# The modulation of a diffusion layer joins the first FFN: two sections ahead of x, six made beside the products

## The reference

```python
mod = (silu(c) @ ada_w + ada_b).reshape(1, 9, 1024)        # once with c_ctx, once with c; ada_w is 1024 x 9216
h = rmsnorm(x, norm_w[0]) * (1.0 + m[1]) + m[0]
x = x + 0.5 * m[2] * swiglu(h, ffn1_w13, ffn1_w2)          # (silu(h @ a) * (h @ b)) @ d, hidden width 2816
h = rmsnorm(x, norm_w[1]) * (1.0 + m[4]) + m[3]
x = x + m[5] * token_mixer(h)                              # projection, RWKV-7 scans, Fourier mixing, merge
h = rmsnorm(x, norm_w[2]) * (1.0 + m[7]) + m[6]
x = x + 0.5 * m[8] * swiglu(h, ffn2_w13, ffn2_w2)
```

## Time and profile before

| | us |
|---|---|
| median of the runs shown | 3244.37 (3243.7 to 3245.0) |
| profiled execution, its own time | 3243.18 |
| span of its profile | 3241.4 |
| PE busy | 2975.2 (92%) |
| DVE busy | 1456.3 (45%) |
| ACT busy | 776.3 (24%) |
| POOL busy | 332.4 (10%) |

### The profile page before, as it was taken

One profiled execution on the slowest core, in us unless ns is written; L12 is line 12 of the kernel. 1 busy time (PEld: TensorE's weight loads), 2 busy tenths in 40 slices (PEclk: granted clock), 3 DMA queues, 4 the chain that ended last, 5 costly groups with the idle time before them and its releaser, 6 DMA issues. The chain is left out here.

```text
span 3241.4 us, 56108 instructions
## 1 busy us (share of the span) xinstructions
PE 2975.2 (92%) x23416; PEld 2787.4 (86%) x23416; DVE 1456.3 (45%) x2475; ACT 776.3 (24%) x1296; POOL 332.4 (10%) x318
## 2 busy tenths in 40 slices
PE   4799999999996999998699976989979999999997
PEld 1399999999995988998588954779879999999996
DVE  0344333334436345432688855335553343443335
ACT  0321111111113233443133334212141111111112
POOL 0310000000004001122121212012240000000000
PEclk7899999999998999999799998989999999999999
DMA  9411111111102334443444321242111111111111
GB/s 399 159 40 39 39 39 39 57 50 42 39 13 90 129 107 149 164 156 138 116 109 96 68 107 33 71 172 93 44 36 46 39 39 39 39 39 39 39 40 64
DMA packets 182217, 263.72 MB, mean 81 GB/s; under 512 B 78128, under 2 KB 133424, under 8 KB 177456
## 3 DMA queue, kind: packets, MB, share of 16 engines
q1 hardware_dynamic: 182064, 261.52, 24.5%
HBM read 206.35 MB, written 55.12 MB: 81 GB/s over the span
## 5 line engine op out<-in xcount | busy, mean ns | idle before, releaser
L474 DVE SCALAR_TENSOR_TENSOR x<-bank,gate,x 128x128 f32<-128x128 f32 (+1 forms) x832 | 411.6, 516 | 209.6 <-PE bank L573 209.1
L609 DVE TENSOR_TENSOR g_ffn<-act_out_ffn,bank 128x384 f32<-128x384 f32 x132 | 73.2, 554 | 742.7 <-ACT act_out_ffn L606 742.7
L558 PE MATMUL bank<-h_hi_ffn,wlo_a_ffn 128*128 128x384 f32 x1056 | 356.9, 338 | 21.2 <-DVE h_lo_ffn L325 11.3
L606 ACT ACTIVATE act_out_ffn<-bank 128x384 f32<-128x384 f32 x132 | 65.0, 492 | 1246.1 <-PE bank L558 1246.0
L558 PE MATMUL bank<-h_lo_ffn,whi_a_ffn 128*128 128x384 f32 x1056 | 355.8, 337 | 0.0
L558 PE MATMUL bank<-h_hi_ffn,whi_a_ffn 128*128 128x384 f32 x1056 | 355.5, 337 | 0.0
L573 PE MATMUL bank<-g_hi_ffn,wlo_d_ffn 128*128 128x384 f32 x1056 | 352.9, 334 | 2.4 <-DVE g_lo_ffn L494 2.4
L573 PE MATMUL bank<-g_hi_ffn,whi_d_ffn 128*128 128x384 f32 x1056 | 352.7, 334 | 0.0
L558 PE MATMUL bank<-h_hi_ffn,whi_b_ffn 128*128 128x384 f32 x1056 | 352.7, 334 | 0.0
L573 PE MATMUL bank<-g_lo_ffn,whi_d_ffn 128*128 128x384 f32 x1056 | 352.7, 334 | 0.0
L558 PE MATMUL bank<-h_hi_ffn,wlo_b_ffn 128*128 128x384 f32 x1056 | 352.7, 334 | 0.0
(11 more groups left out here) (236 smaller groups left out, 4915.9 us busy)
## 6 DMA issues: line engine op xcount, KB each, us to landing
ada_raw<-in_ada_w SPq DMA_DIRECT2D x36, 1024.0 KB, 11.6
raw_a_ffn<-in_ffn_w SPq DMA_DIRECT2D x44, 512.0 KB, 4.6
raw_b_ffn<-in_ffn_w SPq DMA_DIRECT2D x44, 512.0 KB, 4.5
raw_d_ffn<-in_ffn_w SPq DMA_DIRECT2D x44, 512.0 KB, 3.6
raw_in<-in_w_in SPq DMA_DIRECT2D x35, 512.0 KB, 5.1
mix<-row_out SPq DMA_DIRECT2D x23, 576.0 KB, 3.1
sc_ar<-streams SPq DMA_DIRECT2D x36, 256.0 KB, 3.5
sc_bkv<-streams SPq DMA_DIRECT2D x36, 256.0 KB, 4.2
```

Source lines behind the costliest of these rows:

```text
L474: ins = nc.vector.scalar_tensor_tensor(xs, kit.banks[4 + d % 4][:, a:b], kit.gate[:, gate, d, cond:cond + 1], xs, ALU.mult, ALU.add)
L558: mm = nc.tensor.matmul(kit.banks[2 * slot + j][:, 0:CH], w[q][:, par, cols], v[:, k, toks], start=(k == 0 and m == 0), stop=(k == ku - 1 ...
L606: return self.nc.scalar.activation(out, a, ACT.Silu)
L609: self.nc.vector.tensor_tensor(g32, act_out, b, ALU.mult).then_inc(g32_ready, 1)
```

## The change

The stage `modulation` goes. A class `Opening`, a `Norm` with the modulation in it, takes its place in the first FFN alone; other stages are built as before.

- SP: vectors, select, section 0, section 1, x, a and b of the first tile, section 2, and (behind a wait for section 2's row products) d of the first tile.
- Sections 0 to 2 are made as before, by row products, copies and turns. Squares start when both first sections are turned (the rows lie in the squares' buffer), each waiting for its pair of x blocks. ACT's order is: squares of chunk 0, root 0, the first weights, squares of chunk 2, roots 1 and 2, then h for all chunks. The row products of section 2 stand behind the column sums, its turn behind the first up step.
- Sections 3 to 8 don't use the row products. POOL makes them in 24 units, one for each section and quarter of 256 columns: `acc[p, cond, col]` is the sum over k of `raw[p, col] * silu[p, k, cond]`, 8 multiplications and 7 additions of 128x512. POOL issues its own loads, 128 KB each (192 in all, two buffers, two ahead). There are four sum buffers. In pairs 3 to 8, behind up (0, 2) and up (1, 0), PE sums two quarters each over the partitions, with one-column matmuls against ones into free columns of bank 7, and DVE adds the bias for the pair's section behind up (1, 0). Behind pair 8 DVE forms the remaining scales and gates.

The core of the diff; buffers and semaphores are left out:

```diff
-def modulation(kit):
...
+class Opening(Norm):
+    QW = D // 4
+    SUMS = {(0, 2): (0, 1), (1, 0): (2, 3)}
+    AT = 384
+    TURN_BANK = (7, 4, 7)
...
+    def load_first(self, sp):
+        kit = self.kit
+        sp.dma_start(kit.vec[:], kit.dram["vec"]).then_inc(self.S["vec_loaded"], 16)
+        sp.dma_start(self.select[:], kit.dram["select"]).then_inc(self.S["select_loaded"], 16)
+        for i in range(2):
+            self.load_section(sp, i)
+        for k in range(KT):
+            sp.dma_start(kit.x[:, k, :], kit.dram["xT"][k]).then_inc(self.x_loaded[k // 2], 16)
+
+    def load_third(self, sp):
+        self.load_section(sp, 2)
+        sp.wait_ge(self.S["mod_rows_done"], 6)
...
+    def tensor(self, pe):
+        pe.wait_ge(self.S["silu_ready"], 4)
+        self.rows_of(pe, 0, (0, 1))
+        self.rows_of(pe, 1, (2, 3))
+        pe.wait_ge(self.S["select_loaded"], 16)
+        self.turn(pe, 0)
+        self.turn(pe, 1)
+        pe.wait_ge(self.S["ones_ready"], 3)
+        pe.wait_ge(self.S["section_added"], 2)
+        super().tensor(pe)
+        pe.wait_ge(self.rms_ready, 3)
+        self.rows_of(pe, 2, (5, 6))
...
+    def sum_up(self, pe, i, quarters, x_added):
+
+        pe.wait_ge(x_added, i * 24)
+        for q in quarters:
+            pe.wait_ge(self.S["unit_ready"], i * 4 + (q - 11))
+            for mt in range(2):
+                for cond in range(2):
+                    at = self.AT + 2 * (2 * q + mt) + cond
+                    mm = self.nc.tensor.matmul(self.kit.banks[7][:, at:at + 1], self.acc[:, q, cond, mt * P:(mt + 1) * P],
+                                               self.kit.ones[:, 0:1], start=True, stop=True)
+            mm.then_inc(self.S["unit_turned"], 1)
...
+    def scalar(self, act, split_weights):
...
+        self.copy_rows(act, 0, (0, 1))
+        self.copy_rows(act, 1, (2, 3))
+        act.wait_ge(S["mod_turned"], 2)
+        self.squares(0, act, 0)
+        act.wait_ge(S["ones_ready"], 3)
+        root(0)
+        split_weights()
+        self.squares(0, act, 2)
+        for c in (1, 2):
+            root(c)
+        act.wait_ge(S["scale_ready"], 1)
+        for m in range(NC * KT):
...
+    def sections(self, pool):
+
+        nc, S, QW = self.nc, self.S, self.QW
+        pool.wait_ge(self.h_ready, NC * KT)
+        pool.wait_ge(S["mod_turned"], 3)
+        pool.wait_ge(S["silu_ready"], 4)
+        units = [(i, q) for i in range(3, 9) for q in range(4)]
+
+        def load(n):
+            u, k = divmod(n, KT)
+            i, q = units[u]
+            pool.dma_start(self.raw[:, n % 2], self.kit.dram["ada_w"][i, k // 2, :, k % 2, q * QW:(q + 1) * QW])\
+                .then_inc(self.unit_loaded[n % 2], 16)
+        load(0)
+        load(1)
+        step = 0
+        for u in range(len(units)):
+            if u >= 4:
+                pool.wait_ge(S["unit_turned"], u - 3)
+            acc = self.acc[:, u % 4]
+            for k in range(KT):
+                n = KT * u + k
+                pool.wait_ge(self.unit_loaded[n % 2], 16 * (n // 2 + 1))
+                if step:
+                    pool.wait_ge(S["unit_step"], step)
+                nc.gpsimd.tensor_tensor(self.product[:] if k else acc,
+                                        self.raw[:, n % 2:n % 2 + 1].broadcast_to([P, 2, QW]),
+                                        self.silu[:, k].rearrange("p (c t) -> p c t", t=1).broadcast_to([P, 2, QW]),
+                                        ALU.mult).then_inc(S["unit_step"], 1)
+                step += 1
+                pool.wait_ge(S["unit_step"], step)
+                if n + 2 < KT * len(units):
+                    load(n + 2)
+                if k:
+                    ins = nc.gpsimd.tensor_tensor(acc, acc, self.product[:], ALU.add).then_inc(S["unit_step"], 1)
+                    step += 1
+            pool.wait_ge(S["unit_step"], step)
+            pool.sem_inc(S["unit_ready"], 1)
...
@@ def hidden_stage
+            if opening:
+                opening.load_first(sp)
+            for q in "ab":
                 load(q, 0, True)
+            if opening:
+                opening.load_third(sp)
+            load("d", 0, True)
...
                         up(i, par, c, early)
+                        if opening and early and (par, c) == (0, 0):
+                            opening.third_turn(pe)
+                        if beside and (par, c) in opening.SUMS:
+                            opening.sum_up(pe, i, opening.SUMS[par, c], x_added)
+                        if opening and (early or beside) and (par, c) == (1, 1):
+                            pe.wait_ge(opening.S["section_added"], 3 if early else i + 1)
                         if (par, c) in DOWN:
...
         with kit.stage():
-            modulation(kit)
-        with kit.stage():
-            ffn(kit, "ffn1", 0, "ffn1_w13", "ffn1_w2")
+            ffn(kit, "ffn1", 0, "ffn1_w13", "ffn1_w2", first=True)
```

More of the change, by code:

```diff
@@ L379, in hidden_stage @@
             moving = [(norm_part.h_hi, norm_part.h_lo)] * 2
+            opening = norm_part if norm_part.opens else None
         else:
             norm_part = None
[L382 to L384 removed]
+        g_hi1, g_lo1 = buf("g_hi1", [P, NC, CH], F32R), buf("g_lo1", [P, NC, CH], F32R)
+        if opening:
+            opening.beside(buf)
+        elif norm_part:
             buf("past_scratch", [P, norm_part.scratch_width - 2 * NC * CH])
@@ L387, in hidden_stage @@
         raw = {q: buf(f"raw_{q}", [P, width[q]]) for q in "ab"}
+        whi, wlo = ({q: buf(f"{n}_{q}", [P, 2, width[q]], F32R) for q in "ab"} for n in ("whi", "wlo"))
+        if opening:
+            with ExitStack() as scratch:
+                opening.third(scratch)
+        g_hi, g_lo = [buf("g_hi0", [P, NC, CH], F32R), g_hi1], [buf("g_lo0", [P, NC, CH], F32R), g_lo1]
         raw_d = buf("raw_d", [P, ahead, D])
         raw_of = lambda q, slot: raw_d[:, slot % ahead] if q == "d" else raw[q][:]
-        whi = {q: buf(f"whi_{q}", [P, 2, width[q]], F32R) for q in kinds}
-        wlo = {q: buf(f"wlo_{q}", [P, 2, width[q]], F32R) for q in kinds}
+        whi["d"], wlo["d"] = buf("whi_d", [P, 2, D], F32R), buf("wlo_d", [P, 2, D], F32R)
         act_out, g32 = buf("act_out", [P, 2, CH]), buf("g32", [P, 2, CH])
@@ L405, in load @@
                     combine.load(sp, f, slot, first, g32_ready)
-            for q in kinds:
+            if opening:
+                opening.load_first(sp)
+            for q in "ab":
                 load(q, 0, True)
+            if opening:
+                opening.load_third(sp)
+            load("d", 0, True)
             if load_x:
@@ L486, in step @@
                                g32[:, slot], g32_ready)
+                if opening and early and (par, c) == (0, 2):
+                    opening.third_gate(dve)
                 if (par, c) in DOWN:
@@ L506, in _, with pair @@
                 first_weights()
-            def pair(i, early=False, last=False):
+            def pair(i, early=False, last=False, beside=False):
                 for par in range(2):
@@ L511, in pair @@
                         step(i, par, c, early, last)
+                        if beside and (par, c) == (1, 0):
+                            opening.add_section(dve, i)
             pair(0, early=True)
-            with dve.Fori(1, pairs - 1) as i:
-                pair(i)
+            if opening:
+                with dve.Fori(1, 3) as i:
+                    pair(i)
+                with dve.Fori(3, 9) as i:
+                    pair(i, beside=True)
+                opening.finish(dve)
+                with dve.Fori(9, pairs - 1) as i:
+                    pair(i)
+            else:
+                with dve.Fori(1, pairs - 1) as i:
+                    pair(i)
             pair(pairs - 1, last=True)
@@ L522, in _ @@
                 norm_part.pool(pool)
+            if opening:
+                opening.sections(pool)
             if not combine.on_pool:
@@ L575, in down, with pair @@
                     mm.then_inc(down_done, 1)
-            def pair(i, early=False):
+            def pair(i, early=False, beside=False):
                 for par in range(2):
@@ L585, in _ @@
             pair(0, early=True)
-            with pe.Fori(1, pairs) as i:
-                pair(i)
+            if opening:
+                with pe.Fori(1, 3) as i:
+                    pair(i)
+                with pe.Fori(3, 9) as i:
+                    pair(i, beside=True)
+                with pe.Fori(9, pairs) as i:
+                    pair(i)
+            else:
+                with pe.Fori(1, pairs) as i:
+                    pair(i)
             down(pairs - 1, NC - 1)
```

190 lines of the change are left out of this document (188 added, 2 removed).

## The result

| | median of the runs | profiled execution | span |
|---|---|---|---|
| before | 3244.68 us (3243.7 to 3245.76, 4 runs) | 3243.2 us | 3241.4 us |
| after | 3334.66 us (3331.56 to 3335.94, 4 runs) | 3335.9 us | 3334.1 us |

The changed kernel takes 1.0276 times as long (95% interval 1.0258 to 1.0294), 90 us more. The forecast was 3326 us, 82 us more.

A forecast was written before the change was run, and what follows sets the result against it. TensorE, 92% busy, was taken to bound the kernel, with loading limiting its opening. Opening -83.3, GpSimd-paced pairs +163, clock +2 gave +82 on 3243.2: 3325 us, 3326 as median; range 3195 to 3405 for 8 in 10.

The forecast's parts named there:

- The mechanism: Pairs 4 to 8: TensorE stops once per pair, about 30 us, awaiting GpSimd's units; lower clock behind it.
- The opening: Everything before the first product, reordered: first product at 66.0 instead of 149.28 us, saving 83.3 us, 8 us either way.
- t: GpSimd's time for one unit of sections 3 to 8: 27.2 us, from 18.9 to 36.6; break-even 23.1.
- The issue: GpSimd's own DMA issue, eight per unit: 0.85 us each, ends 0 and 1.85.
- the sum: First t's terms, 27.2 us; later the whole forecast: -83.3 + 163 + 2 = +82, 3325 us, median 3326.
- VectorE's disturbance: VectorE's two-input SBUF subtractions slowing GpSimd's units: 1 us on a unit, 0 to 1.5.
- Landings: GpSimd's loads in the units: issued 4.8 us ahead of use, 128 KB landing in 2.4 us, so not late.
- the stretch of the units: Pairs 3 to 8: 20 units take 545.5 us against 382.7 before, 163 more, plus 2 for the clock.
- Keeping up: Rival, pairs 3 to 8: t 18.9 to 20.2, TensorE never stopped, 3183 to 3190 us; keeping up or nearly, 0.25.
- The hold-up of issues: Rival, GpSimd's units: VectorE delays issues to 1.85 us, t 35.2, 3486 us; 0.13 together with slow landing.
- the slow landing: Rival, GpSimd's loads: landing sets the pace; at 6 us, t 32, 3422 us; 0.13 together with held-up issues.
- The late first product: Rival, opening: chunk 0 waits for the last root, first product near 74, 3334 us; no chance of its own.

The follow-up runs named there:

- one_k: The changed kernel with only the first of eight multiplications per GpSimd unit, one load, no additions; sums and waits kept: 3200.74 us, ratio 0.9859 to the kernel before.
- double_issue: The changed kernel with each of GpSimd's 192 loads issued as two halves, same bytes in 384 issues: 3413.79 us, ratio 1.0518 to the kernel before.
- spread_two_k: The changed kernel with three units a pair in pairs 1 to 8, three sum buffers, and 96 loads of 256 KB: 3201.34 us, ratio 0.9864 to before.
- before_split: The kernel before with TensorE's loop over the first FFN's pairs cut into the changed kernel's three loops, nothing added: 3248.19 us, ratio 1.0009.
- before_order: The kernel before with its weight halves laid out in the changed kernel's order: 3246.81 us, ratio 0.9996.

## Why the prediction was right, point by point

**The mechanism was the predicted one.** A stop once a pair in pairs 4 to 8, ahead of the one-column matmuls, none in pair 3 because four units lie ready, the lower clock behind each, and GpSimd without a gap but for its waits. one_k shows that it is GpSimd's work, double_issue that each microsecond of it counts 20 times. The stops themselves are 17 to 25 us and not the 30 forecast, since a pair's excess also holds the sums, the lower clock and the slower up products.

**The opening, -83.3 forecast, -78.6 measured.** The first product stands at 70.57, not 66.0. The timeline of the kernel after shows where:

```profile
29.50 4.73 PE L300 MATMUL bank<-select,square_n 128*128 128x2 f32 x32
34.27 0.94 ACT L128 ACTIVATE square_n<-x 128x384 f32<-128x384 f32 x2 [4.03 <-PE bank L300]
34.93 8.73 PE L140 MATMUL bank<-square_n,ones 128*128 128x384 f32 x20 [0.71 <-ACT square_n L128]
42.46 1.28 ACT L366 ACT_TABLE_LOAD   x1 [2.69 <-PE bank L140]
43.75 0.58 ACT L366 ACTIVATE inv_rms_n<-bank,eps 128x384 f32<-128x384 f32 x1
47.05 3.57 POOL L132 TENSOR_TENSOR square_n<-x 128x384 f32<-128x384 f32 x2 [0.33 <-PE bank L140]
52.33 1.17 ACT L128 ACTIVATE square_n<-x 128x384 f32<-128x384 f32 x2 [5.29 <-PE bank L140]
58.16 1.85 ACT L383 ACTIVATE h_hi_ffn<-x_normed_n,mod,scale 128x128 fp32r<-128x128 f32 x4
```

```profile
34.00:44.00 10.00, 8.96 (x22) 4.62 (x21) 3.63 (x7) 3.52 (x6) 2.45 (x4) 0.76 1.02 424
```

The turns took 4.73 us instead of 3.9, yet the squares start on time, 34.27 against 34.4. The column sums of chunk 0 ran at a granted clock of 0.76 and end at 42.46 instead of 39.7. The first root, with 1.28 us for its table load where 0.6 had stood for both, ends at 44.33 instead of 40.3, but h doesn't wait for that: its path goes on through the sums. Chunk 1's last two squares take GpSimd 3.57 us beside VectorE's weight subtractions, ScalarE waits 5.29 us before it can go on with chunk 2's squares, at 52.33, and behind them and the two roots h starts 4.4 us late. Its eight steps add nothing to that. Mostly for the clock 8 us had been left; 4.6 were used, about half of them in chunk 0's column sums. The queue behaved as worked out: its engines were full until 44 us.

**t, 27.2 forecast, 26.7 measured**, but not term by term. With no VectorE instruction beside them the multiplications took 1.04 us instead of 1.16 and the additions 1.29 instead of 1.28. VectorE's disturbance, forecast at 1 us a unit, was 0.8: with it the means are 1.12 and 1.32. Each of the 21 arithmetic instructions above 1.5 us ran beside one of VectorE's weight subtractions. (The pair called undisturbed in the earlier trace rows wasn't: `x_normed_n`, with two SBUF inputs, ran beside it.) The issue took 0.58 us instead of 0.85, mis-sized by a third; what made up for it is a wait of 0.30 us ahead of each one for the multiplication that it stands behind, where the forecast had 0.08. An issue between two dependent instructions thus costs 0.9 us, and the sum held by errors that cancelled, which is luck. Landings, held to be hidden, cost 10.7 us in 24 units.

The Trainium skill, SBUF — State Buffer (SBUF: two separate sides), names about 620 ns for a DMA issued from GpSimd alone, by which, taken as the issue's price, the sum had been 3290 us, an estimate. The issue's record is near that, 578 ns, and the measurement lies 45 us above the sum. The 3100 ns that the prediction cites with it hold beside a DVE copy, and VectorE makes no copy in this stretch, so no run here tests them: 190 of the 192 issues took 0.58 or 0.59 us (the first two, one behind the other, 0.72 and 0.54), 25 of these 190 beside a VectorE subtraction of two SBUF inputs.

**What the sum left out**: slower up products (2.5 + 0.3 + 2.1 us outside the stops; inside them they are hidden, like the sums, 3.3 us a pair where 3.9 had been forecast), 1.9 and 1.3 us up to the scans, 5.2 us in the scans and 1.4 behind them. Together with the stretch of the units (156.6 against 163 + 2) and the opening this gives the 92.7 us between the two spans: 8 us too much in the units' stretch, 5 too little for the opening and 15 left out. That the total came within 9 us is thus in part luck. The scans' 5 us are not shown to be the change's: the scans are 2.4 to 7.0 us longer in the traces of all kernels with GpSimd's loads, but also 5.9 us longer in that of before_split, which has none of them, and 1.5 in that of before_order. No run says why they vary.

**The rivals.** Keeping up would have needed t under 20.2; it did not occur, and in spread_two_k TensorE isn't stopped because each pair asks for three units, not four, and a unit has half the issues. The hold-up of issues and the slow landing (2.6 us for 128 KB on the page after) did not occur. The late first product did occur, for its half.

## What to carry to other kernels

When an idle engine is given a side job, compare its time per loop iteration with that of the engine that will wait for it, waits between its own dependent instructions included: here four units of 26.7 us met a pair of 79. A ring lets it run ahead by its depth once, not in every iteration; so spread the job over as many iterations as there are, make its instructions and issues fewer and larger, and only then count the main engine's share. The gain of the opening was real, 79 to 85 us; it was lost to stops of 134 us, which spreading the same work over two more pairs took away.

## What was not expected of the hardware

- A DMA issued from GpSimd costs that engine 0.58 us for 128 KB, 0.75 for 256 KB, 0.53 for the second of two of 64 KB in a row, and 0.30 us of waiting if it stands behind an arithmetic instruction that it needs; another arithmetic instruction waits 0.08 to 0.15.
- A GpSimd multiplication of 128x512 whose inputs both repeat took 1.04 us, an addition with two full inputs 1.27 to 1.31. Beside VectorE's 128x1024 subtractions of two SBUF inputs they took up to 1.88 us, and these subtractions up to 2.83 us instead of 1.22.
- A matmul of 384 columns at full clock takes 176.5 or 173.2 ns in the same loop, in kernels that differ in where its two operands lie: 103520 and 103552 bytes apart it was the slower, 101888, 103936 and 105984 apart the faster. These last are all multiples of 512. One execution with 106080 was slower and the median of that kernel was not, so it isn't settled that the distance is the reason.
